# The first panels of a feed-forward group in buffers of their own, and a modulation fold one tile later

## The reference

```python
def reference(x, c, ...):
    x = layer_norm(x, ln_in_g, ln_in_b)
    c_act = jax.nn.silu(c)
    for l in range(DEPTH):          # DEPTH = 1
        ada = (c_act @ w_ada[l] + b_ada[l]).reshape(c.shape[0], 3, 3, D_MODEL)
        mod = lambda i, j: ada[:, i, j][:, None, :]
        h = x * (1.0 + mod(0, 1)) + mod(0, 0)
        x = layer_norm(ALPHA * x + 0.5 * mod(0, 2) * swiglu(h, ffn1_w_in[l], ffn1_w_out[l]), ln1_g[l], ln1_b[l])
        h = x * (1.0 + mod(1, 1)) + mod(1, 0)
        y = token_mixer(h, ...)     # pooling and three-branch attention, two branch products, gates, @ w_mix_out
        x = layer_norm(ALPHA * x + mod(1, 2) * y, ln2_g[l], ln2_b[l])
        h = x * (1.0 + mod(2, 1)) + mod(2, 0)
        x = layer_norm(ALPHA * x + 0.5 * mod(2, 2) * swiglu(h, ffn2_w_in[l], ffn2_w_out[l]), ln3_g[l], ln3_b[l])
    return x
```

## Time and profile before

| | |
|---|---|
| three timed runs | 1113.32, 1116.38, 1116.26 us |
| their median | 1116.26 us |
| the profiled execution's own time | 1114.81 us |
| its span, first to last instruction | 1113.0 us |
| PE busy | 1103.3 us, 99% of the span |
| DVE, ACT, POOL busy | 522.8, 411.4, 531.0 us |
| mean granted clock of PE | 0.998 |

### The profile page before, as it was taken

One profiled execution on the slowest core, in us unless ns is written; L12 is line 12 of the kernel. 1 busy time (PEld: TensorE's weight loads), 2 busy tenths in 40 slices (PEclk: granted clock), 3 DMA queues, 4 the chain that ended last, 5 costly groups with the idle time before them and its releaser, 6 DMA issues.

```text
span 1113.0 us, 15322 instructions
## 1 busy us (share of the span) xinstructions
PE 1103.3 (99%) x5568; PEld 901.3 (81%) x5568; DVE 522.8 (47%) x896; ACT 411.4 (37%) x654; POOL 531.0 (48%) x275
## 2 busy tenths in 40 slices
PE   9999999999999999999999999999999999999998
PEld 6788888888888997875578887898888888888887
DVE  5667756441121269268757677784222223111113
ACT  5462332323222284278632233267223232222222
POOL 2335544444454464469825453556444444444440
PEclk9999999999999999999999999999999999999999
DMA  9545555322333262210146653314333332233322
GB/s 373 196 163 200 191 178 176 122 94 84 92 101 104 74 256 97 86 41 18 49 134 204 212 198 114 133 58 151 133 113 113 126 113 100 90 87 103 89 68 76
DMA packets 52371, 142.11 MB, mean 128 GB/s; under 512 B 5728, under 2 KB 11872, under 8 KB 51040
## 3 DMA queue, kind: packets, MB, share of 16 engines
q1 hardware_dynamic: 51312, 136.25, 36.8%
q10 hardware_dynamic: 1008, 5.17, 1.2%
HBM read 139.31 MB, written 2.10 MB: 127 GB/s over the span
## 4 chain that ended last, share of the span: by engine, by line
PE 84%; issue 9%; POOL 4%; DVE 2%; ACT 1%; POOLq 0%; DVEq 0%; ACTq 0%
PE psum L644 25%; PE psum L646 25%; PE psum L645 25%; POOL w_lo L555 4%; PE psum L1012 2%; PE psum L1063 1%; PE psum L1091 1%; PE psum L947 1%; PE psum L674 1%; POOL Pr L599 0%; PE psum L726 0%; PE psum L897 0%; PE psum L983 0%; PE psum L748 0%; DVE X L1984 0%
## 5 line engine op out<-in xcount | busy, mean ns | idle before, releaser
L555 POOL TENSOR_TENSOR w_lo<-raw,w_hi 128x1024 fp32r<-128x1024 f32 x183 | 451.8, 2472 | 519.7 <-ACT w_hi L1187 519.3
L644 PE MATMUL psum<-h_hi,w_hi 128*128 128x512 f32 (+1 forms) x1008 | 382.0, 379 | 1.2 <-POOL h_lo L604 1.0
L645 PE MATMUL psum<-h_lo,w_hi 128*128 128x512 f32 (+1 forms) x1008 | 378.7, 376 | 0.0
L646 PE MATMUL psum<-h_hi,w_lo 128*128 128x512 f32 (+1 forms) x1008 | 378.6, 376 | 0.0
L1187 ACT ACTIVATE w_hi<-raw 128x1024 fp32r<-128x1024 f32 x183 | 191.8, 1051 | 147.8 <-PE psum L646 95.8
L644 PEld LDWEIGHTS psum<-h_hi,w_hi 128*128 128x128 f32 x1008 | 189.6, 188 | 41.7 <-issue 4.5
L646 PEld LDWEIGHTS psum<-h_hi,w_lo 128*128 128x128 f32 x1008 | 189.6, 188 | 34.7
L645 PEld LDWEIGHTS psum<-h_lo,w_hi 128*128 128x128 f32 x1008 | 189.7, 188 | 33.7
L1835 DVE SCALAR_TENSOR_TENSOR acc<-ada_raw,cact,acc 128x512 f32<-128x512 f32 x98 | 137.1, 1435 | 15.1 <-DMA ada_raw<-in_ada_w 15.0
L644 PE MATMUL psum<-act_hi,w_hi 128*128 128x512 f32 (+1 forms) x374 | 141.2, 378 | 0.0
L646 PE MATMUL psum<-act_hi,w_lo 128*128 128x512 f32 (+1 forms) x374 | 140.8, 377 | 0.0
(11 more groups left out here) (260 smaller groups left out, 1008.5 us busy)
## 6 DMA issues: line engine op xcount, KB each, us to landing
raw<-in_ffn_in SPq DMA_DIRECT2D x82, 512.0 KB, 3.2
ada_raw<-in_ada_w SPq DMA_DIRECT2D x112, 256.0 KB, 3.5
raw<-in_ffn_out SPq DMA_DIRECT2D x32, 448.0 KB, 3.3
raw<-in_mix_w SPq DMA_DIRECT2D x27, 512.0 KB, 3.3
ada_first<-in_ada SPq DMA_DIRECT2D x8, 1024.0 KB, 10.6
raw<-in_ffn_out SPq DMA_DIRECT2D x16, 512.0 KB, 3.5
raw<-in_branch_w SPq DMA_DIRECT2D x8, 512.0 KB, 3.7
raw<-in_mixout_w SPq DMA_DIRECT2D x8, 512.0 KB, 3.3
```

The costliest lines, as they stand in the source:

```text
L555: gp.tensor_tensor(w_lo[:, slot, :], raw[:, slot % 2, :], w_hi[:, slot, :].bitcast(F32), ALU.subtract).then_inc(split_done, 1)
L644: pe.matmul(o_, w_hi[:, wslot, ws], xh, start=first, stop=False)
L645: pe.matmul(o_, w_hi[:, wslot, ws], xl, start=False, stop=False)
L646: return pe.matmul(o_, w_lo[:, wslot, ws], xh, start=False, stop=last)
```

## The change

Two parts. First, panels 2 to 4 of the group get buffers of their own, `group_hi` and `group_lo`, in a place that the branches' inputs leave free once all branch panels are used. ACT copies one of them ahead of each of the three first-half squares, POOL subtracts all three ahead of the norm's low parts, and the group's products read them there. Second, the fold of the modulation stands behind the projection's tile 0 instead of ahead of it. SP's program is as before.

```diff
@@ buffers
+        group_hi = at("group_hi", [P, GROUP - 1, 1024], R + 57344, F32R)
+        group_lo = at("group_lo", [P, GROUP - 1, 1024], R + 73728, F32R)
@@ gpsimd
+            def group_split(i):
+                p = B_FFN2 + 1 + i
+                gp.wait_ge(split_hi, p + 1)
+                gp.tensor_tensor(group_lo[:, i, :], raw[:, p % 2, :], group_hi[:, i, :].bitcast(F32),
+                                 ALU.subtract).then_inc(split_done, 1)
...
-                    splits(B_BRANCH + 4, end + 3)
+                    splits(B_BRANCH + 4, end + 1)
+                    for i in range(GROUP - 1):
+                        group_split(i)
                 for m in (1, 2, 3, 4):
                     low(L, 0, m)
-                split(end + 3, 3)
+                if L == 1:
+                    split(end + 3, 3)
@@ tensor, group
+                        apart = L == 2 and k >= 2
                         for m in range(GROUP):
-                            ins = product(psum[:, GROUP_BANK[L][m], part(h)], k // 2, GROUP * (k % 2) + m,
-                                          h_hi[:, k, part(h)], h_lo[:, k, part(h)], k == 0, k == KT - 1)
+                            ins = product(psum[:, GROUP_BANK[L][m], part(h)], k // 2 - apart, GROUP * (k % 2) + m,
+                                          h_hi[:, k, part(h)], h_lo[:, k, part(h)], k == 0, k == KT - 1,
+                                          (group_hi, group_lo) if apart else (w_hi, w_lo))
@@ tensor, output projection
             pe.wait_ge(br_mixed, KT - 1)
-            sum_modulation(2, 3, 6)
             for m in range(LATE[2][0]):
...
                 ins.then_inc(panels_used, 1)
+                if m == 0:
+                    sum_modulation(2, 3, 6)
@@ scalar
             def split(p, slot, filled):
                 act.wait_ge(raw_landed[slot % 2], 16 * filled)
+                if isinstance(p, int) and 0 < p - B_FFN2 < GROUP:
+                    act.wait_ge(panels_used, B_MIXOUT)
+                    act.activation(group_hi[:, p - B_FFN2 - 1, :], raw[:, slot % 2, :], ACT.Copy).then_inc(split_hi, 1)
+                    return
...
                 for i in range(late):
+                    if L == 2:
+                        split_before(p0 - 1 + i)
                     square_half(L, i, 0)
```

More of the change, by code:

```diff
@@ L640, in _, with product @@
         def _(pe):
-            def product(o_, wslot, kk, xh, xl, first, last):
+            def product(o_, wslot, kk, xh, xl, first, last, w=(w_hi, w_lo)):
                 ws = slice(kk * P, (kk + 1) * P)
-                pe.matmul(o_, w_hi[:, wslot, ws], xh, start=first, stop=False)
-                pe.matmul(o_, w_hi[:, wslot, ws], xl, start=False, stop=False)
-                return pe.matmul(o_, w_lo[:, wslot, ws], xh, start=False, stop=last)
+                pe.matmul(o_, w[0][:, wslot, ws], xh, start=first, stop=False)
+                pe.matmul(o_, w[0][:, wslot, ws], xl, start=False, stop=False)
+                return pe.matmul(o_, w[1][:, wslot, ws], xh, start=False, stop=last)
             def panel_over_h(p, wslot, b, h_wait=None):
```

## The result

The kernel became slower. The median of 11 runs is 1119.32 us (1117.78 to 1122.02) against 1113.85 us of 11 runs of the kernel before (1113.20 to 1116.38); the ratio is 1.0044, with an interval of 1.0035 to 1.0052, so 4.9 us, 3.9 to 5.8. The profiled execution took 1119.19 us, with a span of 1117.4.

The account below looks back on a forecast made before the run. TensorE, busy 99% of the span, was taken to bound the kernel. Fold +0.24, stall +3.7 and group -0.85 made +3.1 us, added to 1115.5 us: 1118.6 us, range 1114.9 to 1122.3.

Parts of the forecast that it names:

- slower was the likeliest side: Chances for the measured time against the kernel before: slower 0.50, within about 0.3% 0.44, faster 0.06.
- a change of +3.1: Whole kernel: +0.24 + 3.7 - 0.85 = +3.1 us, ends +1.5 and +4.8; the forecast had chance 0.60.
- The gap gives nothing: Ahead of projection tile 0: moving the fold gains nothing, as the product waits for GpSimd's split; bounds 0 and 0.1 us.
- +0.24 for the fold's passes: Behind projection tile 0: the fold's two passes now stand in a dense TensorE stream, +0.24 us, bounds 0.2 and 0.3.
- +3.7 for the stall: At the half norm's transposes near 725: TensorE waits 3.7 us for VectorE's sums, bounds 3.0 and 4.5.
- The two chains: Ahead of the transposes: panel 4's copy and VectorE's addition beside panel 3's split delay the sums, to 728.7 and 728.95.
- the chain through panel 4: Panel 4, issued after GpSimd splits panel 2, is copied ahead of the last square; sum done at 728.7, 0.25 us earlier.
- -0.85 for the group: Second feed-forward layer's group: splits gone and VectorE's addition 0.42 instead of 1.27 us, ending 0.85 us earlier; bounds 0 and 1.7.
- The clock: Behind the stall: rival that the granted clock falls, losing 1.6 us more, so +4.7 us, 1120.2 us; chance 0.22.
- The fall at the kernel's end: Kernel's end: clock at 0.51 over 3.30 us after 3.32 us of small matmuls; taken as agreeing with the skill's rule.
- The third rival: Projection's third tile: the fold's small VectorE pass, held through both GpSimd splits, costs 0.7 us; +3.8, 1119.3 us; chance 0.06.

Follow-up runs that it names:

- e1: The kernel before with only the fold moved behind the projection's tile 0: median 1114.86 us, ratio 1.0013 (1.0004 to 1.0022).
- e8: The kernel before with the fold behind tile 0 and nine extra unused products in the gap ahead of tile 0: median 1114.75 us, ratio 1.0004.
- e5: The changed kernel with only panel 4's copy moved, from ahead of the third half square to behind the root: one execution, 1119.21 us.
- e6: The changed kernel with panel 4's copy behind the root and the second half square written to PSUM: one execution, 1115.42 us.
- e7: The changed kernel with panel 2's copy still ahead of the first square, panels 3 and 4's behind the third square and the root: one execution, 1113.17 us.
- e2: The changed kernel with the fold back ahead of tile 0, so the group's part alone: median 1118.39 us, ratio 1.0039.
- e3: The changed kernel with the fold back ahead of tile 0 and each panel copy two squares later: median 1114.09 us, ratio 0.9997.
- e4: The changed kernel with 24 extra unused products ahead of the first half's transposes, filling the stall: median 1119.22 us, ratio 1.0039.
- e10: The changed kernel, fold back ahead of tile 0, with 5 extra unused products in the gap and 24 ahead of the transposes: median 1118.36 us, ratio 1.0027.

## Why the prediction came out as it did

The time, 1119.32 us, lies in the range, 0.7 us above the forecast; slower was the likeliest side. That the forecast came so near is in part luck. It was a base of 1115.5 us, from four times, and a change of +3.1. The base was 1.65 us above the 1113.85 that 11 runs gave, and the change came out at 4.9 (3.9 to 5.8), so 1.8 us larger than forecast: two errors of opposite sign. By the steps:

- **The gap gives nothing.** Right: 2.03, 1.99 and 2.12 us from branch to projection before, in e1 and after. GpSimd's split of that panel was named as the releaser. The traces of e1 and after write "issue" there, but that of e8, with the fold moved too and TensorE kept busy in the gap, names it:

```profile
686.93 0.50 PE L644 MATMUL psum<-mixed_hi,w_hi 128*128 128x512 f32 x1 [0.47 <-POOL w_lo L555]
```

- **+0.24 for the fold's passes.** Right in the trace: after tile 0's last product at 694.01 the fold stands at 694.24 and the next product but one at 694.69 instead of 694.46. What I hadn't priced is the emptied gap: the fold's matmuls had stood in it, and the clock fell behind it in the execution of the filled stall, though not in after, e1, e5, e6 or e7. The fold alone is missing more clock than the same with its gap filled (2.8 against 2.1), but with 11 and 12 runs this isn't outside chance. Open.
- **+3.7 for the stall.** 3.53 was measured (4.2 in e2 and 3.7 in e5, by the same reading). The two chains, the landings behind GpSimd's splits and the hold of VectorE were there as worked out; e3, e5 and e6 each took links away; the stall went to nothing, stayed, and fell to 1.3 us, as each link's worth would have it. That the chain through panel 4 was the later one, not the other, changes nothing in the size.
- **-0.85 for the group.** -0.83 was measured, in every kernel with early splits; the addition at 739.53 takes 0.41 in place of 1.27 us, and the ten steps 16.2 in place of 17.0.
- **The clock.** This is the term that was missing from the sum of +3.1. It stood as a rival at 0.22, priced 1.6 us, because the clock had held in the stretch of 2.30 us ahead of tile 0. It fell in all three profiled executions with a long, unfilled stall (3.5 us in after, 4.2 in e2, 3.7 in e5), for 3.3 us at 0.50, and cost 1.50 in after. With the stall filled (e4, e10) it held there. Behind the stall of 1.3 us (e6) it held. So it belonged in the likeliest sum: +4.7 against 4.9 measured. By the fit it cost 1.2 us on average rather than 1.5, so it may spare some executions, or one fall may stand for another that would have come anyway. The rule of the Trainium skill that was weighed there ("TensorE: Matmul & The Clock Gate", section "HAM oscillation — how this bites in real kernels") was the better guide than the one gap in the trace that spoke against it. From start to start that gap was 2.03 us, with the fold's matmuls in it, against 2.95 us with nothing in it at the stall, and another 0.89 to the second pair of transposes. The fall at the kernel's end, which the prediction called agreement with that rule, is another case: TensorE counted as busy for 3.26 of the 3.32 us ahead of it.
- **The third rival.** VectorE's small pass was held by GpSimd, 1.65 us from 695.42, but through one split only. The residual behind it ends at 697.85, well ahead of the third tile: no cost, as the text had for that case.

## What to carry to other kernels

Work that is moved ahead on an in-order engine takes its waits along: put a copy that waits for a transfer behind the last instruction that the bounding engine needs, not ahead of it. Add to a long stall of the bounding TensorE what the fall of the clock behind it takes (3.5 us of wait became 5.0 here), and don't argue from a shorter gap that went unpunished. Look for a fall at the same place in several executions before calling it mended: at the kernel's end it stayed away in five of eleven by itself. Where VectorE and GpSimd both read SBUF, an addition can take as long as GpSimd's whole pass; one input in PSUM frees it.

## What the runs showed of the hardware

- The runs of one kernel lie on steps of about 1.4 us. Of the 60 spans of the kernel before, 16 lie at 1111.0 to 1111.8 us, 31 at 1112.6 to 1113.8, 11 at 1114.1 to 1114.9, two above, and none between. The mean clock goes with the step, though not strictly: 1.000 in 8 of the lowest and 0.998 in 6 of them. In the profiled executions it goes with the number of falls: 1.000 with none (e1, e7), 0.997 or 0.998 with one (before, e2, e3, e6, e8), 0.996 or 0.997 with two (after, e4, e5), 0.994 with three (e10). A few of these make more scatter than most edits here are worth.
- Falls come elsewhere than behind long waits too, and in some executions only. At about 14 to 17.4 us the clock fell in after, e4 and e10 and in none of the other nine, behind the same short matmuls and a wait of 0.9 us. Behind small matmuls of two columns at the end it fell in six of the eleven without fillers there.
- VectorE's scale of 8 columns with a single SBUF input took 1.65 us beside GpSimd's split, so the hold isn't confined to two inputs. Why a pass that small is held was not tried.
